# Three changes to a fused two-block kernel: one-pass gates, one-pass mean shift, and two bias rows loaded from the on-chip row

## The chip, the core and the metric

The kernel runs on one core of a Trainium2 chip. The metric is the device time of one execution in microseconds. Three executions of the kernel before took 2050.70, 2051.24 and 2051.36 us; the median is 2051.24. The profiled execution took 2050.76 us, of which the span from the first to the last instruction is 2048.9.

## What is computed

Two transformer blocks over 512 tokens of width 1024, all in float32. The parts that the change touches are these.

```python
# block 1: gated linear attention, its gates
log_a = log_sigmoid(g_low @ gla_gate_up + gla_gate_bias) / 16     # g_low: 512 x 16, gate_up: 16 x 512
# block 2, two layers: forgetting attention
log_f = log_sigmoid(f_logit + b_forget)                            # 512 x 8 heads
c = cumsum(log_f, axis=tokens)
logits = where(causal, scores + c[query] - c[key], -inf)           # per head
# block 2, after each half layer
mu = mean(x); var = mean(square(x - mu)); y = (x - mu) * rsqrt(var + eps) * g + b
```

The rest is projections, a block attention, a retention part and feed-forward products.

## The kernel before

Activations stand transposed: eight tiles of 128 channels by 512 tokens. TensorE does the large products as three one-pass products. A weight tile and an activation tile are each split into a high part, which the one-pass type float32r holds, and the low rest, and high*high + high*low + low*high is summed in PSUM (`tile`, L675 to L692, and `tile_tok`, L706 to L717). ScalarE makes the high parts of weights (L2135) and VectorE the low parts (L1273), a piece of 8 x 128 columns at a time, and `Walk` keeps pieces prepared two ahead. SyncE loads the weights into two stage buffers (L2851), each when the pieces of the buffer's old content are split.

One Python walk is run for each engine, with the same order of steps. A *tick* is one step k of a product, three matmuls. Side work (an attention, the linear attention, a norm's mean) is a generator in `w.beside`; each tick adds `w.pace` to a credit, and each whole credit runs one step of the generator. So a `yield` more is a step later on every engine. Engines work in program order, and semaphores in `on.wait_ge` hold them back.

**Gates.** After the last thin product, VectorE adds its two halves into `glow` (16 x 512), scales it (L1471), and TensorE computes the gates of one head with one float32 matmul, `gup` times `glow` (L871), four times, in steps of `gla` at pace 0.55. ScalarE and VectorE turn each into the decay factors.

**Mean shift.** The norm of block 2 keeps its sums exact by first taking off a rough mean. `norm_tile` copies tile 0 to `accq` (L1757) and adds tiles 1 to 7 (L1760) as they come. After tile 1, in the third step, `centre` multiplies the sum of two tiles by a matrix of 1/1024 in float32 (L1001), and ScalarE scales the result by 4 into `cB`, which `deviate` subtracts (L1770). There are four norms, N = 0 to 3: N = 0 and 2 behind the output product of layers 0 and 1, N = 1 and 3 behind the feed-forward product. In `last_three`, more sums and the normalisation follow.

**Bias of the forgetting attention.** VectorE makes the negative running sum of the eight heads, `lsb`, 8 partitions x 512. GpSimd writes it to `cneg` in memory (L2813), waits, and loads for each head its row, repeated over 128 partitions, into `Cb` (`load_cb`, L2803 to L2807; issue at L2806), heads 0 and 1 at once and the next ones as buffers come free. Of it and of the columns in `stat` it makes the bias of each of 32 score tiles in `bi` (L2822, L2826). VectorE adds the bias to the scores and takes the maximum (L1309), which frees the two score banks of TensorE (L774, L775); ScalarE takes the exponential (L2172), and after the normalisation and TensorE's transpose it copies the high part of the turned tile into `x_PT` (L2181). The first such additions stand on VectorE ahead of the low halves of the value tiles (L1359), and these free the banks in which the next products of TensorE begin (L686). A store of the eight tiles of H (`parked`, L2861) must be over before `Cb` is written, since they share room.

Of the kernel before, what the change touches and what calls it, by code (L numbers as in the profile page):

```python
# [7 lines left out]
F32 = mybir.dt.float32  # L8
# [487 lines left out]
def build(nc, xT, w_in, gate_up, w_bm, w_bg, w_out, w_up, w_down, w_in2, w_out2, w_ff1, w_ff2,  # L496
          consts, params, out, vrev, cneg):
    ctx = ExitStack()
    with ctx:
        base = -(-nc.sbuf_base // 64) * 64  # L500

        def at(name, off_kb, shape, dt=F32):
            return nc.alloc_sbuf_tensor_at(name, shape, dt, offset=base + int(off_kb * KB))
# [48 lines left out]
        ones = at("ones", g0 + 1, [128, 128])  # L552
        onec = at("onec", g0 + 1.5, [128, 128])
        onev = at("onev", g0 + 2, [128, 128])
# [9 lines left out]
        H = at("H", g0 + 12, [128, 8, S])  # L564
        ident, blk = cst[:, 0:128], cst[:, 128:256]
        epsc, eps5, rtok, mqs = rcol[:, 8:9], rcol[:, 9:10], rcol[:, 0:4], rcol[:, 10:11]
# [5 lines left out]
        oh = at("oh", g0 + 66, [33, 640])  # L572
        gup = at("gup", g0 + 92, [16, 512])
        sq = [at("sq0", g0 + 80, [128, S]), at("sq1", g0 + 82, [128, S])]
# [16 lines left out]
        rev = at("rev", g0 + 69, [128, 640])  # L591
        glow = at("glow", g0 + 94, [16, 512])

# [19 lines left out]
        d8 = at("d8", g0 + 36, [128, 8, S])  # L613
        acc2 = at("acc2", g0 + 70, [128, S])
        cB = at("cB", g0 + 72, [128, S])
        muB = at("muB", g0 + 74, [128, S])
# [52 lines left out]
        def tensor(e):  # L669
# [199 lines left out]
            def gates(hd):  # L869
                on.wait_ge(gup_in["in"], vec_gla["low"], *free[4])  # L870
                t = e.matmul(banks[4][:, :], gup[:, 128 * hd:128 * hd + 128], glow[:, :], start=True, stop=True)  # L871
                t.then_inc(*pe_gla.up("gate", hd))
                free[4] = [vec_gla["z", hd]]
                yield
                yield

            def gla():
                for _ in range(2):
                    yield
# [119 lines left out]
            def centre(N):  # L999
                on.wait_ge(vec_norm["acc", N, 1], *free[4])  # L1000
                t = e.matmul(banks[4][:, :], onec[:, :], accq[:, :], start=True, stop=True)  # L1001
                t.then_inc(*pe_sum.up("centre", N))
                free[4] = [act_norm["centre", N]]
# [260 lines left out]
        def vector(e):  # L1264
# [126 lines left out]
            e.tensor_copy(gmask[:, :], cm2[:, 0:128]).then_inc(*vec_x.up("gmask"))  # L1391
            e.tensor_scalar(mqs, prm[:, V_MQ:V_MQ + 1], 0.125, None, ALU.mult).then_inc(*vec_x.up("mqs"))

            moba = Heads(0)
# [66 lines left out]
            def ev_thin(dst, *events):  # L1461
# [7 lines left out]
                return evict  # L1469
            w.thin("P", nothing, ev_thin(glow[:, :]))  # L1470
            e.tensor_tensor(glow[:, :], glow[:, :], rB[0:16, :], ALU.mult).then_inc(*vec_gla.up("low"))  # L1471

# [36 lines left out]
            def gla():  # L1509
                for _ in range(2):  # L1510
                    yield
# [242 lines left out]
            def norm_tile(N, j):  # L1754
                if j == 0:
                    on.wait_ge(*h_over[0], *over("norm", N))
                    e.tensor_copy(accq[:, :], H[:, 0, :]).then_inc(*vec_norm.up("acc", N, 0))  # L1757
                else:
                    on.wait_ge(*h_over[j], vec_norm["acc", N, j - 1], *([pe_sum["centre", N]] if j > 1 else []))
                    e.tensor_tensor(accq[:, :], accq[:, :], H[:, j, :], ALU.add).then_inc(*vec_norm.up("acc", N, j))  # L1760
                if j == 1:
                    w.beside.append(spaced([nothing], 3))
                    w.pace = 1.0
                for k in DEVIATE.get(j, ()):
                    deviate(N, k, None)
# [359 lines left out]
        def scalar(e):  # L2125
# [148 lines left out]
            def ev_val(m):  # L2274
                return lambda i, c, b: w.after(2, lambda: qk_square(m))
# [7 lines left out]
            for what, j in MOBA_TILES:  # L2283
                w.gemm("P", 8, nothing, ev_val(j) if what == "val" else nothing)
            for half in range(2):
                w.tok("P", nothing, nothing)
            w.finish()
            w.thin("P", nothing, nothing)


# [18 lines left out]
            def gla():  # L2309
                for _ in range(2):  # L2310
                    yield
# [181 lines left out]
            def centre(N):  # L2493
                on.wait_ge(pe_sum["centre", N], *over("norm", N))
                t = e.activation(cB[:, :], banks[4][:, :], ACT.Copy, scale=4.0)
                t.then_inc(*act_norm.up("centre", N))
# [108 lines left out]
            for L in range(2):  # L2605
# [29 lines left out]
                def first_heads(L=L, a=a, fox=fox, ph=ph):  # L2635
                    w.beside.append(attention_order(w, fox, Attention(
                        a, fpS, fPT, [cneg_out["out", L], vec_attn["sums", L], *ph[0]], [parked["out", L]])))

# [108 lines left out]
        def gpsimd(e):  # L2747
# [52 lines left out]
            for L in range(2):  # L2800
# [10 lines left out]
                duplicate(a, 1 - L, *began)  # L2811
                on.wait_ge(vec_attn["cneg", L])
                e.dma_start(cneg[L], lsb).then_inc(*cneg_out.up("out", L, by=16))  # L2813
                load_cb(0, parked["out", L])
                load_cb(1, parked["out", L])
                for n in range(32):
# [138 lines left out]
```

## Time and profile before

| | before |
|---|---|
| median of three | 2051.24 us |
| profiled execution | 2050.76 us |
| its span | 2048.9 us |
| TensorE busy | 2024.0 us, 99% |
| VectorE, ScalarE, GpSimd busy | 64%, 50%, 18% |
| granted clock of TensorE, mean | 0.998 |
| float32 gates, L871 | 8 records for 4 matmuls |
| float32 shifts, L1001 | 8 records for 4 matmuls |

How to read it: an engine's busy time is the union of its records. TensorE's matmuls are pipelined, so a record of 0.39 us with the next one 0.23 us later is the usual picture; the cost of a matmul is read between starts. An idle time stands only where TensorE had nothing in flight.

### The profile page before, as it was taken

The page shows a single profiled execution, that of the slowest core. Times are in us where ns is not written, and L with a number is a line of the kernel's source. Part 1 is how long each engine was busy: PE and PEld are TensorE (multiplying, and loading weights), DVE is VectorE, ACT ScalarE, POOL GpSimd, SP SyncE. Part 2 cuts the span into 40 slices and gives each one's busy share as a digit, 9 for nine tenths or more (in the row PEclk, how much of TensorE's full clock was granted, in tenths as well). Part 3 has the DMA queues.
Part 4 walks back from the last instruction along what each step waited for, and adds up shares of the span by engine and source line. Part 5 has one row for each costly group of instructions (what it writes and reads, how often), then busy time and mean ns, then how long its engine had stood idle before and what let it go on. Part 6 is the DMA issues. An engine that isn't in the chain of part 4 may idle for free. (4 is left out here: it accounts for less than half of the span.)

```text
span 2048.9 us, 27766 instructions
## 1 busy us (share of the span) xinstructions
PE 2024.0 (99%) x11040; PEld 1730.9 (84%) x11040; DVE 1302.5 (64%) x2058; ACT 1020.7 (50%) x1684; POOL 371.3 (18%) x315
## 2 busy tenths in 40 slices
PE   9999999999999999999999999999999999999997
PEld 6888788888898998788788899898888788899896
DVE  6664656566774664476677575567677577566576
ACT  5664344334462543366357364464566357364363
POOL 0010000000133230254000233130354000323220
PEclk9999999999999999999999999999999999999999
DMA  7332222423232423633232242332533332242331
GB/s 245 98 108 64 83 62 83 143 95 111 90 117 73 133 66 100 181 103 103 98 104 85 81 144 62 105 122 63 166 110 90 115 93 95 65 143 62 124 104 41
DMA packets 201533, 211.58 MB, mean 103 GB/s; under 512 B 7803, under 2 KB 181115, under 8 KB 201404
## 3 DMA queue, kind: packets, MB, share of 16 engines
q1 hardware_dynamic: 194544, 194.13, 30.4%
q0 software_dynamic: 6352, 15.24, 2.8%
q8 instruction: 87, 1.43, 0.3%
q10 hardware_dynamic: 508, 0.43, 0.1%
q14 instruction: 42, 0.34, 0.1%
HBM read 194.55 MB, written 8.95 MB: 99 GB/s over the span
## 5 line engine op out<-in xcount | busy, mean ns | idle before, releaser
L686 PE MATMUL ps<-Phi,wh 128*128 128x512 f32 (+1 forms) x888 | 352.9, 397 | 3.8 <-DVE x_fvv L1359 1.3
L1273 DVE TENSOR_TENSOR wl<-stage,wh 128x1024 fp32r<-128x1024 f32 (+1 forms) x246 | 311.8, 1274 | 60.8 <-ACT wh L2135 42.1
L689 PE MATMUL ps<-Phi,wl 128*128 128x512 f32 (+1 forms) x888 | 332.1, 374 | 0.6 <-DVE wl L1273 0.6
L687 PE MATMUL ps<-Plo,wh 128*128 128x512 f32 (+1 forms) x888 | 331.4, 373 | 0.0
L2135 ACT ACTIVATE wh<-stage 128x1024 fp32r<-128x1024 f32 (+3 forms) x249 | 248.1, 1009 | 61.8 <-PE ps L689 38.9
L686 PE MATMUL ps<-Qhi,wh 128*128 128x512 f32 (+1 forms) x664 | 253.0, 381 | 0.7 <-DVE Qlo L1292 0.7
L687 PE MATMUL ps<-Qlo,wh 128*128 128x512 f32 (+1 forms) x664 | 251.6, 379 | 0.0
L689 PE MATMUL ps<-Qhi,wl 128*128 128x512 f32 (+1 forms) x664 | 251.5, 379 | 0.0
L2760 POOL TENSOR_TENSOR ws<-stage 128x1024 f32<-128x1024 f32 x20 | 54.9, 2744 | 932.2 <-PE ps L689 619.7
L686 PEld LDWEIGHTS ps<-Phi,wh 128*128 128x128 f32 x888 | 167.7, 189 | 41.0 <-issue 11.6
L689 PEld LDWEIGHTS ps<-Phi,wl 128*128 128x128 f32 x888 | 167.2, 188 | 31.8 <-DVE wl L1273 1.0
L687 PEld LDWEIGHTS ps<-Plo,wh 128*128 128x128 f32 x888 | 167.8, 189 | 27.7 <-issue 4.1
L1737 DVE TENSOR_TENSOR H<-H,ps 128x512 f32<-128x512 f32 x74 | 50.8, 687 | 175.8 <-PE ps L689 175.8
L686 PE MATMUL ps<-Qhi,wxh 128*128 128x512 f32 (+1 forms) x424 | 153.3, 362 | 0.0
L687 PE MATMUL ps<-Qlo,wxh 128*128 128x512 f32 (+1 forms) x424 | 151.4, 357 | 0.0
L689 PE MATMUL ps<-Qhi,wxl 128*128 128x512 f32 (+1 forms) x424 | 151.4, 357 | 0.0
L686 PEld LDWEIGHTS ps<-Qhi,wh 128*128 128x128 f32 x664 | 124.9, 188 | 25.3 <-DVE Qlo L1292 1.5
L687 PEld LDWEIGHTS ps<-Qlo,wh 128*128 128x128 f32 x664 | 124.9, 188 | 23.7 <-issue 0.5
L689 PEld LDWEIGHTS ps<-Qhi,wl 128*128 128x128 f32 x664 | 124.9, 188 | 23.5
L1292 DVE TENSOR_TENSOR Qlo<-f,Qhi 128x512 fp32r<-128x512 f32 x96 | 82.3, 857 | 68.6 <-ACT Qhi L2152 68.6
L1273 DVE TENSOR_TENSOR wxl<-stage,wxh 128x1024 fp32r<-128x1024 f32 (+1 forms) x90 | 116.9, 1303 | 7.3 <-ACT wxh L2135 7.2
L2135 ACT ACTIVATE wxh<-stage 128x1024 fp32r<-128x1024 f32 (+1 forms) x90 | 85.3, 964 | 36.7 <-PE ps L689 21.3
(357 smaller groups left out, 4579.2 us busy)
## 6 DMA issues: line engine op xcount, KB each, us to landing
stage<-in_w_ff SPq DMA_DIRECT2D x64, 1024.0 KB, 5.4
stage<-in_w_in SPq DMA_DIRECT2D x39, 1024.0 KB, 5.2
stage<-in_w_up SPq DMA_DIRECT2D x16, 1024.0 KB, 5.4
stage<-in_w_down SPq DMA_DIRECT2D x16, 1024.0 KB, 5.0
stage<-in_w_in SPq DMA_DIRECT2D x30, 512.0 KB, 5.2
stage<-in_w_out SPq DMA_DIRECT2D x12, 1024.0 KB, 5.0
stage<-in_w_bg SPq DMA_DIRECT2D x4, 1024.0 KB, 5.0
vrev<-H SPq DMA_DIRECT2D x2, 2048.0 KB, 14.4
```

Source lines behind the costliest of these rows:

```text
L686: e.matmul(o, hi[:, k, cs_], hi_x[:, kx, tok], start=k == 0, stop=False)
L687: e.matmul(o, hi[:, k, cs_], lo_x[:, kx, tok], start=False, stop=False)
L689: t = e.matmul(o, lo[:, k, cs_], hi_x[:, kx, tok], start=False, stop=k == nk - 1)
L1273: t = e.tensor_tensor(lo, src, hi.bitcast(F32), ALU.subtract)
L1292: t = e.tensor_tensor(lo, src, hi.bitcast(F32), ALU.subtract)
L1737: t = e.tensor_tensor(H[:, j, :], H[:, j, :], banks[b][:, :], ALU.add)
L2135: e.activation(hi, src, ACT.Copy).then_inc(*w_high.up(i))
L2760: e.tensor_tensor(ws[u][:, :, :, :], one, other, ALU.add).then_inc(*pool.up("weights", i))
```

## The change

It does three things.

1. The gates. `gup` and `glow` get copies of 80 rows in float32r, with 16 rows each at 0, 32 and 64 and zeros between: `gup3` has high, low, high, `glow3` has high, high, low. One matmul over the 80 rows sums high*high, low*high and high*low. ScalarE makes two copies of each, VectorE one subtraction and one memset of each. The low-rank row is made in `tm1` first. On all engines `gla` begins with four empty steps instead of two.
2. The mean shift. Tile 0 is copied to `first` in float32r (same place as `acc2`), and `centre` multiplies it alone, in one pass, by the matrix in float32r (1/1024); ScalarE scales by 8. The sum in `accq` begins with the addition of tiles 0 and 1.
3. The bias rows. GpSimd issues the load of head 0 straight from row 0 of `lsb`, then the write to `cneg`, then the load of head 1 from row 1 of `lsb`. Heads 2 to 7 load from `cneg` as before. ScalarE's first turned copy into `x_PT` (L2181), which writes over the place of `lsb`, now also waits for both loads.

```diff
@@ -550,7 +550,7 @@
         ones = at("ones", g0 + 1, [128, 128])
-        onec = at("onec", g0 + 1.5, [128, 128])
+        onecr = at("onec", g0 + 1.5, [128, 128], F32R)
@@ -562,7 +562,7 @@
         H = at("H", g0 + 12, [128, 8, S])
-        ident, blk = cst[:, 0:128], cst[:, 128:256]
+        ident, blk, onec = cst[:, 0:128], cst[:, 128:256], onecr[:, :].bitcast(F32)
@@ -570,7 +570,7 @@
         oh = at("oh", g0 + 66, [33, 640])
-        gup = at("gup", g0 + 92, [16, 512])
+        gup3, gup = at("gup3", g0 + 92, [80, 512], F32R), at("gup", g0 + 94, [16, 512])
@@ -589,7 +589,7 @@
         rev = at("rev", g0 + 69, [128, 640])
-        glow = at("glow", g0 + 94, [16, 512])
+        glow3 = at("glow3", g0 + 94, [80, 512], F32R)
@@ -612,6 +612,7 @@
         acc2 = at("acc2", g0 + 70, [128, S])
+        first = at("first", g0 + 70, [128, S], F32R)
@@ -867,15 +868,15 @@
             def gates(hd):
-                on.wait_ge(gup_in["in"], vec_gla["low"], *free[4])
-                t = e.matmul(banks[4][:, :], gup[:, 128 * hd:128 * hd + 128], glow[:, :], start=True, stop=True)
+                on.wait_ge(act_gla["gup"], vec_gla["gup low"], act_gla["low"], vec_gla["low low"], *free[4])
+                t = e.matmul(banks[4][:, :], gup3[:, 128 * hd:128 * hd + 128], glow3[:, :], start=True, stop=True)
...
             def gla():
-                for _ in range(2):
+                for _ in range(4):
@@ -997,8 +998,8 @@
             def centre(N):
-                on.wait_ge(vec_norm["acc", N, 1], *free[4])
-                t = e.matmul(banks[4][:, :], onec[:, :], accq[:, :], start=True, stop=True)
+                on.wait_ge(vec_norm["acc", N, 0], *free[4])
+                t = e.matmul(banks[4][:, :], onecr[:, :], first[:, :], start=True, stop=True)
@@ -1390,6 +1391,7 @@
             e.tensor_scalar(mqs, prm[:, V_MQ:V_MQ + 1], 0.125, None, ALU.mult).then_inc(*vec_x.up("mqs"))
+            e.memset(gup3[:, :].bitcast(F32), 0.0).then_inc(*vec_gla.up("gup zero"))
@@ -1467,8 +1469,17 @@
                 return evict
-            w.thin("P", nothing, ev_thin(glow[:, :]))
-            e.tensor_tensor(glow[:, :], glow[:, :], rB[0:16, :], ALU.mult).then_inc(*vec_gla.up("low"))
+            on.wait_ge(act_gla["gup"])
+            t = e.tensor_tensor(gup3[32:48, :], gup[:, :], gup3[0:16, :].bitcast(F32), ALU.subtract)
+            t.then_inc(*vec_gla.up("gup low"))
+            on.wait_ge(vec_gla["gup low"])
+            e.memset(glow3[:, :].bitcast(F32), 0.0).then_inc(*vec_gla.up("low zero"))
+            glow = tm1[0:16, :]
+            w.thin("P", nothing, ev_thin(glow, *turns_over(0)))
+            e.tensor_tensor(glow, glow, rB[0:16, :], ALU.mult).then_inc(*vec_gla.up("low"))
+            on.wait_ge(act_gla["low"])
+            t = e.tensor_tensor(glow3[64:80, :], glow, glow3[0:16, :].bitcast(F32), ALU.subtract)
+            t.then_inc(*vec_gla.up("low low"))
@@ -1507,7 +1518,7 @@
             def gla():
-                for _ in range(2):
+                for _ in range(4):
@@ -1754,10 +1765,11 @@
                     on.wait_ge(*h_over[0], *over("norm", N))
-                    e.tensor_copy(accq[:, :], H[:, 0, :]).then_inc(*vec_norm.up("acc", N, 0))
+                    e.tensor_copy(first[:, :], H[:, 0, :]).then_inc(*vec_norm.up("acc", N, 0))
                 else:
-                    on.wait_ge(*h_over[j], vec_norm["acc", N, j - 1], *([pe_sum["centre", N]] if j > 1 else []))
-                    e.tensor_tensor(accq[:, :], accq[:, :], H[:, j, :], ALU.add).then_inc(*vec_norm.up("acc", N, j))
+                    before = accq[:, :] if j > 1 else H[:, 0, :]
+                    on.wait_ge(*h_over[j], *([vec_norm["acc", N, j - 1]] if j > 1 else h_over[0]))
+                    e.tensor_tensor(accq[:, :], before, H[:, j, :], ALU.add).then_inc(*vec_norm.up("acc", N, j))
@@ -2282,10 +2294,16 @@
                 w.gemm("P", 8, nothing, ev_val(j) if what == "val" else nothing)
+            on.wait_ge(gup_in["in"], vec_gla["gup zero"])
+            e.activation(gup3[0:16, :], gup[:, :], ACT.Copy).then_inc(*act_gla.up("gup first"))
+            e.activation(gup3[64:80, :], gup[:, :], ACT.Copy).then_inc(*act_gla.up("gup"))
...
             w.thin("P", nothing, nothing)
+            on.wait_ge(vec_gla["low"])
+            e.activation(glow3[0:16, :], tm1[0:16, :], ACT.Copy).then_inc(*act_gla.up("low first"))
+            e.activation(glow3[32:48, :], tm1[0:16, :], ACT.Copy).then_inc(*act_gla.up("low"))
@@ -2307,7 +2325,7 @@
             def gla():
-                for _ in range(2):
+                for _ in range(4):
@@ -2492,7 +2510,7 @@
                 on.wait_ge(pe_sum["centre", N], *over("norm", N))
-                t = e.activation(cB[:, :], banks[4][:, :], ACT.Copy, scale=4.0)
+                t = e.activation(cB[:, :], banks[4][:, :], ACT.Copy, scale=8.0)
@@ -2634,7 +2652,7 @@
                     w.beside.append(attention_order(w, fox, Attention(
-                        a, fpS, fPT, [cneg_out["out", L], vec_attn["sums", L], *ph[0]], [parked["out", L]])))
+                        a, fpS, fPT, [cneg_out["out", L], Cb_in[0][L, 0], Cb_in[1][L, 1], vec_attn["sums", L], *ph[0]], [parked["out", L]])))
@@ -2809,10 +2827,12 @@
                 duplicate(a, 1 - L, *began)
-                on.wait_ge(vec_attn["cneg", L])
-                e.dma_start(cneg[L], lsb).then_inc(*cneg_out.up("out", L, by=16))
-                load_cb(0, parked["out", L])
-                load_cb(1, parked["out", L])
+                on.wait_ge(vec_attn["cneg", L], parked["out", L])
+                for h in range(2):
+                    src = bass.AP(tensor=lsb.tensor, offset=S * h, ap=[[S, 1], [0, 128], [1, S]])
+                    e.dma_start(Cb[h][:, :], src).then_inc(*Cb_in[h].up(L, h, by=16))
+                    if h == 0:
+                        e.dma_start(cneg[L], lsb).then_inc(*cneg_out.up("out", L, by=16))
```

## Rows read from the trace of the kernel before

**Rows 1.** The page, section 1: busy us (share of span) xinstructions, by engine.
```profile
PE 2024.0 (99%) x11040; PEld 1730.9 (84%) x11040; DVE 1302.5 (64%) x2058; ACT 1020.7 (50%) x1684; POOL 371.3 (18%) x315
```

**Rows 2.** TensorE timeline, 211:214, around the gate: start, us, engine, line, op, shapes, count.
```profile
211.24 0.39 PE L689 MATMUL ps<-Phi,wl 128*128 128x512 f32 x1
...
211.69 0.39 PE L687 MATMUL ps<-Plo,wh 128*128 128x512 f32 x1
211.92 0.39 PE L689 MATMUL ps<-Phi,wl 128*128 128x512 f32 x1
...
213.62 0.40 PE L687 MATMUL ps<-Plo,wh 128*128 128x512 f32 x1
```

**Rows 3.** Timeline of TensorE, 2002 to 2005, around the fourth shift (L1001, not shown).
```profile
2002.39 0.39 PE L689 MATMUL ps<-Qhi,wxl 128*128 128x512 f32 x1
...
2003.71 0.40 PE L687 MATMUL ps<-Qlo,wxh 128*128 128x512 f32 x1
```

**Rows 4.** Timeline, 1654.5 to 1658: VectorE's copy, TensorE's third shift, in brackets idle and releaser.
```profile
1654.64 0.43 DVE L1757 COPY accq<-H 128x512 f32<-128x512 f32 x1
...
1655.06 0.39 PE L689 MATMUL ps<-Qhi,wl 128*128 128x512 f32 x1
...
1655.85 1.12 PE L1001 MATMUL ps<-accq,onec 128*128 128x512 f32 x2 [0.40 <-DVE accq L1760]
...
1657.04 0.40 PE L687 MATMUL ps<-Qlo,wh 128*128 128x512 f32 x1
```

**Rows 5.** Timeline of VectorE, 1040 to 1110, after the first shift.
```profile
1054.90 0.69 DVE L1734 SCALAR_TENSOR_TENSOR H<-H,ps 128x512 f32<-128x512 f32 x1 [0.55 <-PE ps L689]
```

**Rows 6.** Timeline of GpSimd, 850 to 872 and 1455 to 1482.
```profile
852.77 0.54 POOL L2813 DMA_DIRECT2D cneg<-x_z  x1 [7.88 <-DVE x_z L1968]
854.85 1.14 POOL L2806 DMA_DIRECT2D x_Cb<-cneg  x2 [1.54 <-DMA cneg<-x_z]
860.05 0.60 POOL L2822 TENSOR_SCALAR x_bi<-x_Cb,stat 128x128 f32<-128x128 f32 x1 [4.06 <-DMA x_Cb<-cneg]
...
1462.38 0.54 POOL L2813 DMA_DIRECT2D cneg<-x_z  x1 [8.94 <-DVE x_z L1968]
1466.09 1.14 POOL L2806 DMA_DIRECT2D x_Cb<-cneg  x2 [3.17 <-DMA cneg<-x_z]
1471.04 0.60 POOL L2822 TENSOR_SCALAR x_bi<-x_Cb,stat 128x128 f32<-128x128 f32 x1 [3.82 <-DMA x_Cb<-cneg]
```

**Rows 7.** Timelines of VectorE and TensorE, 868 to 869 and 1472 to 1480.
```profile
868.05 0.69 DVE L1359 SCALAR_TENSOR_TENSOR x_fvv<-ps,x_fvv 128x512 fp32r<-128x512 f32 x1
...
868.90 0.46 PE L686 MATMUL ps<-Phi,wh 128*128 128x512 f32 x1
...
1472.66 0.44 PE L774 MATMUL ps<-f0kh,f0qs 128*128 128x384 f32 x1 [0.59 <-DVE stat L1309]
...
1479.88 0.47 PE L686 MATMUL ps<-Phi,wh 128*128 128x512 f32 x1 [1.34 <-DVE x_fvv L1359]
```

**Rows 8.** DMA digits and GB/s in 40 slices: 1445:1465; 102.2:107; 853:854.7.
```profile
DMA  0004589998999999999999999899999999999841
GB/s 0 0 4 41 94 287 311 385 295 193 295 402 393 422 410 414 377 377 377 393 381 373 393 361 307 176 225 234 324 389 348 328 273 270 286 259 270 235 125 45
...
DMA  0000000000798993059997789998999963000000
GB/s 0 0 0 0 0 0 0 0 0 0 171 290 171 188 205 69 0 119 205 256 239 137 154 171 239 239 205 188 222 239 256 188 137 69 17 0 0 0 0 0
...
GB/s 24 12 24 12 0 0 0 0 0 0 0 0 0 0 0 0 0 0 0 0 145 48 49 49 48 0 48 0 0 0 0 0 0 0 0 0 0 0 0 0
```

**Rows 9.** Timelines of SyncE and ScalarE, 854 to 866.
```profile
854.83 1.00 SPq L2851 DMA_DIRECT2D stage<-in_w_in  x2
...
865.30 1.04 ACT L2135 ACTIVATE wh<-stage 128x1024 fp32r<-128x1024 f32 x1
```

**Rows 10.** Timeline of ScalarE, 1480 to 1490.
```profile
1482.28 0.26 ACT L2181 ACTIVATE x_PT<-ps 128x128 fp32r<-128x128 f32 x1
```

## The prediction

> **What bounds the kernel now.** I read the page's busy shares first: TensorE is busy in 99% of the span [rows 1], so a change counts by what it takes off TensorE's own stream, or by what it does to the few gaps in it. Next I read TensorE's timeline at the lines that the change touches, measuring from start to start, because the matmuls' ends are modelled and overlap. Then I read the few rows of TensorE that carry an idle time, and for those the engine that released them: VectorE at two of the four mean shifts [rows 4], and VectorE twice at the start of the second layer's attention [rows 7]. The last view is of the DMA engines, since the change has them read the bias row from another place.
>
> **The gates (four matmuls, L871).** In the plain stream two matmuls take 211.69 - 211.24 = 0.45 us. From the matmul before a gate to the second after it (211.92 to 213.62) is 1.70 us [rows 2]. So an fp32 gate costs 1.70 - 0.45 = 1.25 us. The new gate is one fp32r matmul of the same 512 columns over 80 rows, 0.23 us at the pitch of its neighbours. Saved: 1.02 us each, 4.1 us in all.
> No row shows an fp32r matmul over 80 rows. The fp32 shift over 128 rows costs 2003.71 - 2002.39 - 0.45 = 0.87 us [rows 3], 0.38 less than the gate over 16 rows with the same columns; if that 0.38 is the price of few rows and 80 still count as few, the saving is 1.02 - 0.38 = 0.64 each, 2.6 in all. An end below that has no ground: one pass replaces a product that takes several. I take 4.1, as 80 rows are nearer to 128 than to 16.
> The Trainium skill's page "TensorEngine Tiling (Array Packing)", section "Key Properties", says that changing the tiling mode drains TensorE, and its list of modes has 32, 64 and 128 rows. By that 16 rows fall in another mode than the 128-row stream and 80 don't, and the sum stays as it is; the 0.38 us agrees with a drain, though the row doesn't show its cause.
> What the gates add: on VectorE two memsets, two subtractions of at most 16x512; on ScalarE four copies of 16x512. On either engine that is 0.5 to 0.7 us apiece by their 512-column neighbours. The weights' row splits are done before the attention's tail, and the low-rank row's splits stand between its product and the first gate. For these the first gate now comes two steps later: at 0.55 steps a tick and 0.68 us a tick (three matmuls at 0.23) that is 2.5 us, against two copies and one subtraction, some 2.0 us. I cost them at nothing on TensorE; without that cover it would be a wait of at most 2.0 us once. Behind ScalarE's new wait for the low-rank row stands its next weight piece, behind VectorE's wait for the copies three memsets and the low half of one; TensorE holds two pieces prepared ahead, 5.5 us each.
>
> **The shift (four matmuls, L1001).** An fp32 shift costs 0.87 us in the stream [rows 3], a one-pass one 0.23: 0.64 each, 2.5 us in all. Two of the four also wait: 1655.06 to 1657.04 is 1.98 us where the free one takes 1.32 [rows 4], so 0.66 is a wait for the sum of two tiles; the other (layer 0) is the same to 0.01. Now it waits for the copy alone, which ends at 1655.07 [rows 4], ahead of the 1655.29 at which TensorE is there. If the copy to the one-pass type takes as long as an addition (0.69 instead of 0.43) it is 0.1 us late. Both waits are worth 1.3 us. In layer 0 part of it has no use: VectorE, which everything in the norm goes through next, has only 0.55 us idle before its next tile [rows 5], of 0.64 + 0.66 = 1.3 that TensorE would bring; 0.7 comes back as a wait later. Shift together: 2.5 + 1.3 - 0.7 = 3.1 us. Taking one tile's sum and 8 instead of two and 4 adds no instruction.
> So the two TensorE edits are worth 4.1 + 3.1 = **7.2 us**, between 5 and 8.
>
> **The bias rows (two layers).** GpSimd writes the row to memory at 852.77, issues the two loads when it has landed (854.85) and starts the first bias at 860.05; in layer 1 at 1462.38, 1466.09 and 1471.04 [rows 6]. The change drops the hop: load 0 goes out at 852.77 and 1462.38, then the write to memory, then load 1. Without anything else the first bias comes 2.1 and 3.7 us earlier. What is late next, if so, is nothing: in layer 1 TensorE's idle 0.59 and 1.34 us go [rows 7], in layer 0 there was none.
> But the load now has 128 readers of one partition. Three rows bound what that costs. With all partitions taking part and the engines full (digit 9) they move up to 422 GB/s, some 25 per engine. The copies from 64 partitions to 64 move 188 to 290 at digit 9, mostly near 230, a little over half. The write from 8 partitions runs at 49 GB/s [rows 8]. So the pace falls with the partitions touched. 256 KB (262144 bytes) would take 5.3 us at 49 GB/s, and 43 us if one of the eight partitions gives an eighth of it. Between these ends I take one engine's pace, 25 GB/s, which is 10.4 us: it is also half of what the eight partitions give, and the row nearest to the case is theirs. With 1.8 us for the way (2.1 from issue to use for the write, less 0.3 for its bytes) load 0 is in 12.2 us after its issue: at 865.0 and 1474.6, so 4.9 and 3.5 us **later** than before.
> The Trainium skill's page "SBUF — State Buffer", section "Door 1: The DMA port swizzle", speaks against this edit: eight partitions share one port, and a transfer over partitions 0 to 3 was measured at 27.6 GB/s. That gives an estimate of 9.5 us instead of 10.4 for the row, and a sum 1.8 us lower than mine (0.9 in each layer). The rows on 8 and on 64 partitions agree with it; none here has a single one.
> TensorE feels it through VectorE, which works in order: its bias additions stand ahead of the value tiles that free TensorE's banks. In layer 0 that value tile is done at 868.74 and TensorE needs it at 868.90 [rows 7], 0.1 to 0.2 of cover; in layer 1 it is already late. The price is 4.8 + 3.5 = **8.3 us**. Load 1 lands 10.4 later than load 0. The fifth bias wants it, behind four of GpSimd's, and now ScalarE too, before its first turned copy: in layer 1 at 1482.28 [rows 10] + 3.5 = 1485.8, against 1462.38 + 1.8 + 20.8 = 1485.0. I count it as covered, by 0.8 us; at a slower pace this wait, with the exponentials and value tiles queued behind it, becomes the longer one, and each us on a row costs two. The loads for the heads from 2 on find the row in memory as before. GpSimd's joint wait for the parked tiles isn't new (the load waited for them).
>
> **Sum.** The profiled execution took 2050.76 us (span 2048.9), 0.5 below the median of 2051.24. 2050.8 - 7.2 + 8.3 = 2051.9 on that one, 2052.3 against the median.
>
> **Rivals.**
> A, the row is read as fast as memory (5.2 us from issue to use, as now) or at 49 GB/s (5.3 + 1.8 = 7.1). For it: the engines read repeated rows of memory without trouble. Against it: the half-height copies. Then layer 0 pays nothing and layer 1 gets back its 1.9 us (1.6 at 49 GB/s): 2051.2 - 7.2 - 1.9 = 2042.1.
> B, slower: the readers hold the DMA engines, and the weights wait behind them. Place: weights issued at 854.83 are turned by ScalarE at 865.30 [rows 9], ahead of the value tiles on its queue. The two row loads hold the engines to 852.77 + 1.8 + 2 x 10.4 = 875.4; ScalarE would want the weights at 865.30 + 4.9 = 870.2, so it stands 5.2 us, and in layer 1 about as long. It decides from a landing some 15 us after that issue, instead of before 865. Price 10.4: 2052.3 + 10.4 = 2062.7.
> C, one pass saves less than counted (the first gate waits 2.0 us, or 80 rows still pay): 2054 to 2056, with the row as forecast.
>
> **Chances.** Forecast 0.50, its own range 2048 to 2057; A 0.27; B 0.16; C 0.07. A measurement of this kernel can tell about 0.2%, 4.1 us: faster is below 2047.1, slower above 2055.3. Faster: A's 0.27 and 0.03 of the forecast's low end = 0.30. Slower: B's 0.16, 0.04 of C, 0.13 of the forecast's high end (the row at under 21 GB/s, or half of B) = 0.33. The rest, 0.37, is within 0.2%. The range for 8 in 10 is 2041 to 2062: it takes in A, and B up to its full price. It leaves out a row at an eighth of 49 GB/s.
>
> **What would show it.** Right: gates and shifts with one record of about 0.4 us and 0.45 us to the second matmul after plus 0.23; no idle before a shift in either layer; load 0 of each layer with a landing near 12 us, TensorE idle at the third score product and at the first matmul after the value tiles, 4.8 us in layer 0. Wrong: a landing of 3 to 7 us (A), ScalarE idle on a stage of weights near 870 and 1480 (B), unhidden weight loads around the gates or TensorE idle at the first gate (C). The biggest error to expect is in the 10.4 us: 1 us more in each layer is 2 us of the whole.

## The result, and the profile after

The changed kernel takes 2075.41 us (median of 4, 2074.93 to 2076.61) against 2051.22 us (2050.70 to 2051.36): 24.2 us **slower**, ratio 1.012 (95% interval 1.0108 to 1.0131). The forecast was 2052.3, and the range 2041 to 2062 doesn't hold the time. The profiled execution took 2075.08 us (span 2073.3, mean granted clock 0.993).

The two TensorE edits did on TensorE what they should. First the page's busy times, then TensorE's timeline around the first gate (L872) and the fourth shift (L1002); columns are start, us, engine, line, operation, shapes, count.

```profile
PE 2022.1 (98%) x11032; PEld 1733.5 (84%) x11032; DVE 1305.7 (63%) x2062; ACT 1023.7 (49%) x1688; POOL 369.0 (18%) x315
```

```profile
215.19 0.39 PE L690 MATMUL ps<-Phi,wl 128*128 128x512 f32 x1
215.42 0.40 PE L872 MATMUL ps<-glow,gup 80*128 80x512 f32 x1
215.65 0.40 PE L687 MATMUL ps<-Phi,wh 128*128 128x512 f32 x1
...
2027.17 0.39 PE L690 MATMUL ps<-Qhi,wxl 128*128 128x512 f32 x1
2027.40 0.39 PE L1002 MATMUL ps<-first,onec 128*128 128x512 f32 x1
2027.62 0.39 PE L687 MATMUL ps<-Qhi,wxh 128*128 128x512 f32 x1
2027.85 0.39 PE L688 MATMUL ps<-Qlo,wxh 128*128 128x512 f32 x1
```

The gate over 80 rows takes 0.23 us of the stream, as any matmul of 512 columns (before 1.25 [rows 2]); the shift too (2027.85 - 2027.17 = 0.68, before 1.32 [rows 3]). TensorE is busy for 1.9 us less and yet ends 24.4 later, so it is idle for 26.3 us more. Most of that, 22.6 us, is in four rows, two in each attention, where the kernel before has 0, 0, 0.59 and 1.34 us [rows 7]:

```profile
864.42 0.44 PE L775 MATMUL ps<-f0kh,f0qs 128*128 128x384 f32 x1 [2.78 <-DVE stat L1310]
...
880.17 0.76 PE L687 MATMUL ps<-Phi,wh 128*128 128x512 f32 x1 [9.88 <-DVE x_fvv L1360]
...
1487.67 0.69 PE L775 MATMUL ps<-f0kh,f0qs 128*128 128x384 f32 x1 [3.90 <-DVE stat L1310]
...
1502.88 0.76 PE L687 MATMUL ps<-Phi,wh 128*128 128x512 f32 x1 [7.93 <-DVE x_fvv L1360]
```

The two waits of a pair have different causes. The **first wait** is that of a late bias. GpSimd's timeline in both layers answers to [rows 6]:

```profile
850.92 0.57 POOL L2833 DMA_DIRECT2D x_Cb<-x_z  x1 [7.88 <-DVE x_z L1980]
851.48 0.56 POOL L2835 DMA_DIRECT2D cneg<-x_z  x1
852.01 0.59 POOL L2833 DMA_DIRECT2D x_Cb<-x_z  x1
862.80 0.60 POOL L2842 TENSOR_SCALAR x_bi<-x_Cb,stat 128x128 f32<-128x128 f32 x1 [10.20 <-DMA x_Cb<-x_z]
...
1474.07 0.57 POOL L2833 DMA_DIRECT2D x_Cb<-x_z  x1 [8.93 <-DVE x_z L1980]
...
1486.05 0.60 POOL L2842 TENSOR_SCALAR x_bi<-x_Cb,stat 128x128 f32<-128x128 f32 x1 [10.31 <-DMA x_Cb<-x_z]
```

From GpSimd's first issue to its first bias it is 11.9 and 12.0 us, against 7.3 and 8.7 before: 4.6 and 3.3 us late. The **second wait** is behind ScalarE, which stands on a stage of weights with the value tiles queued behind it:

```profile
876.58 1.06 ACT L2147 ACTIVATE wh<-stage 128x1024 fp32r<-128x1024 f32 x1 [8.43 <-DMA stage<-in_w_in]
...
1499.28 1.06 ACT L2147 ACTIVATE wh<-stage 128x1024 fp32r<-128x1024 f32 x1 [7.90 <-DMA stage<-in_w_in]
```

Before, ScalarE had that stage at 865.30 without a wait [rows 9]. What happened to it is in the DMA view of two stretches of layer 0, 852.9 to 862.4 and 872 to 877 (mean busy share of the 16 engines in tenths, 40 slices, then what they moved; q0 is GpSimd's queue, q1 the one with the weights). It is also in the landing times, that is the time from a load's issue until all of it has arrived, of the row loads (L2833) and of the three weight loads issued from 853 on (L2871):

```profile
DMA  6009699909600596990990056999099000699908
GB/s 17 0 0 34 17 34 69 52 0 52 17 0 0 17 34 17 86 52 0 34 34 0 0 17 17 34 52 86 0 34 34 0 0 9 26 43 52 78 0 26
DMA packets 102, 0.26 MB, mean 27 GB/s; under 512 B 36, under 2 KB 36, under 8 KB 102
q0 software_dynamic: 102, 0.26, 90.5%
...
DMA packets 2346, 1.63 MB, mean 326 GB/s; under 512 B 35, under 2 KB 2345, under 8 KB 2345
```

```profile
DMA to landing us min/median/max: 11.8/15.9/20.1
...
DMA to landing us min/median/max: 12.1/20.9/23.2
```

For 9.5 us all 102 packets are GpSimd's. They take up 90.5% of the time of 16 engines and move 27 GB/s. (The digits have gaps, since a packet of 4 KB is longer than a slice; q0's share is the number to read.) Not one packet of weights moves in that stretch, though two loads of them were issued at its start. Load 0 lands 11.8 us after its issue, load 1 after 20.1, so at 862.7 and 872.1: 9.4 us apart for 256 KB, 28 GB/s. From 862.4 to 870.3 it is much the same: q0 takes 90.8%, and 0.02 MB of weights move. Only as load 1 runs out do the weights come in, 0.3 MB before 872 and 1.63 MB in the 5 us shown, and ScalarE goes on at 876.58.

After the long waits TensorE also runs at its lower clock for a while. The stretches 866 to 870, 870 to 880, 880 to 883 and 883 to 890 (busy time and count by engine, then the granted clock, the DMA share, GB/s):

```profile
866.00:870.00 4.00, 4.00 (x19) 3.19 (x17) 1.58 (x4) 0.60 (x2) 3.42 (x4) 1.00 0.97 32
870.00:880.00 10.00, 0.29 (x2) 0.00 (x0) 2.28 (x5) 2.49 (x5) 0.41 (x1) 0.65 0.73 210
880.00:883.00 3.00, 2.83 (x8) 2.17 (x8) 2.41 (x7) 2.96 (x7) 1.53 (x4) 0.50 0.20 60
883.00:890.00 7.00, 7.00 (x37) 5.85 (x36) 3.57 (x11) 4.18 (x10) 4.58 (x5) 0.99 0.59 162
```

0.50 is the 1.2 GHz level. Matmuls start every 0.43 us there instead of 0.23, seven of them: 1.4 us. In layer 1 it is more, since both waits are followed by such a stretch, again at a granted 0.50: seven matmuls after the 3.90 us and eleven after the 7.93 us. In all TensorE is busy for 5.8 us longer than in e3 below, which has the same one-pass products and the rows through memory (2022.1 against 2016.3).

### The profile page after: what moved, and what is told of

The parts are those of the page before. It is cut to its first block and busy times, and to the rows that moved or that the text cites. A ratio compares the mean times of both kernels' runs of the same rounds, so it can differ in the third digit from the quotient of the medians.

```text
span 2073.3 us, 27759 instructions
## 1 busy us (share of the span) xinstructions
PE 2022.1 (98%) x11032; PEld 1733.5 (84%) x11032; DVE 1305.7 (63%) x2062; ACT 1023.7 (49%) x1688; POOL 369.0 (18%) x315
```

## The experiments

The theory after the result: the loss is the bias rows' alone, with two prices, the late first bias and the DMA engines held by a read of one partition. The rivals: only the lateness, or a disturbance from the one-pass edits. Times are medians in us. What a run from e5 on costs is counted from e3 (2046.82), also where its code differs from the changed kernel's. In e6, e7, e13, e14 and e17 the bias of one or both of the heads 0 and 1 is left out, so they show only time.

| run | what | us | ratio to before (95%) |
|---|---|---|---|
| e1 | gates alone | 2048.51 | 0.9988 (0.9979 to 0.9997) |
| e2 | shift alone | 2049.93 | 0.9992 (0.9983 to 1.0001) |
| e3, e15 | gates and shift | 2046.82, 2046.62 | 0.998 (0.9971 to 0.9988), 0.998 (0.9972 to 0.9989) |
| e4 | bias rows alone | 2079.53 | 1.0138 (1.0124 to 1.0152) |
| e5 | head 0's row alone from the chip | 2056.67 | 1.0029 (1.0018 to 1.004) |
| e6, e14 | both loads from 8 neighbours | 2053.78, 2055.0 (one run) | 1.0014 (1.0005 to 1.0024) |
| e17 | one load from 8 neighbours | 2048.01 (one run) | |
| e13 | both from 8 partitions, 16 apart | 2047.50 | 0.9981 (0.9972 to 0.999) |
| e7 | both from 128 partitions | 2044.69 | 0.9972 (0.9961 to 0.9984) |
| e8 | e3 and two reads nobody waits for | 2069.33 | 1.009 (1.0075 to 1.0105) |
| e9 | e3 and a late first bias | 2055.90 | 1.0026 (1.0017 to 1.0035) |
| e10, e16 | e3, 128 columns from the chip | 2045.92, 2045.45 | 0.9976 (0.9967 to 0.9985), 0.9972 (0.9961 to 0.9983) |
| e11 | e3, 128 columns first, from memory | 2047.41 | 0.9984 (0.9975 to 0.9992) |
| e12 | e3, gates two steps earlier | 2047.99 | 0.9989 (0.998 to 0.9998) |

### Which edit carries the loss (e1 to e4)

e1 takes the parts of the diff that touch `gup`, `glow` and the empty steps of `gla`, e2 those on `first`, `onec` and the scale, e3 both. e4 takes the rest, against the kernel before:

```diff
-                e.dma_start(cneg[L], lsb).then_inc(*cneg_out.up("out", L, by=16))
-                load_cb(0, parked["out", L])
-                load_cb(1, parked["out", L])
+                for h in range(2):
...
+                    e.dma_start(Cb[h][:, :], src).then_inc(*Cb_in[h].up(L, h, by=16))
+                    if h == 0:
+                        e.dma_start(cneg[L], lsb).then_inc(*cneg_out.up("out", L, by=16))
```

> The kernel before with the one-pass gates alone. Theory (from the trace after): a gate costs 0.23 us instead of 1.25, 4.1 us in all, but about 1.3 to 1.6 us comes back as waits for VectorE at the norm products of the last heads (1.08 and 0.26 us idle seen in the trace after): 2051.2 - 2.6 = 2048.6. Rival (my forecast): nothing comes back, 2047.1. Rival 2: the gates bring nothing here, because what follows was bound by VectorE: 2050.5 to 2051.2.

> The kernel before with the one-pass shift alone. Theory: 0.64 us each in four places and two waits of 0.66 us gone, 1.0 back in layer 0 as a wait of the next product of the same norm (L1013): 2051.2 - 2.9 = 2048.3. My forecast was 3.1: 2048.1. Rival: the norms are bound by VectorE in both layers, so it saves under 1 us: over 2050.2.

> Gates and shift in one pass, the bias rows through memory as before. If the whole loss is the rows' (theory): 2051.2 - 5.5 = 2045.7, between 2044.5 and 2047. Rival, the one-pass edits carry a part of the 24 us: above 2051. My forecast for this part was 7.2 us: 2044.0.

> The bias rows of heads 0 and 1 from the chip alone, gates and shift as before. Theory: all of the loss and the part that the other two edits gave back: 2075.4 + 5.5 = 2081, layer 0 and layer 1 each losing 12 to 15 us on TensorE. Rival, my forecast: 8.3 us, 2059.5. Rival 2, TensorE's earlier arrival through the faster gates and shift is what made the waits long, so that part of the loss is missing here: 2070 to 2078.

Measured: -2.4, -1.0, -4.1 and +28.6 us against the kernel before (2050.95 in these runs). The changed kernel stands 28.6 above e3 too. So the rows carry the whole loss, whatever TensorE does elsewhere, and the one-pass edits are a gain of 4.1. In e4 TensorE's four waits are 2.81, 8.23, 3.87 and 7.55 us, as in the changed kernel. e2 was a miss, 1.0 for 2.9. Its trace shows why: TensorE at the next product of the same norm, and ScalarE 10 us ahead of it:

```profile
1071.84 0.80 PE L1014 MATMUL ps<-accq,onec 128*128 128x256 f32 x1 [2.36 <-DVE accq L1794]
...
1061.32 1.06 ACT L2137 ACTIVATE wh<-stage 128x1024 fp32r<-128x1024 f32 x1 [1.85 <-DMA stage<-in_w_ff]
```

That TensorE is ahead doesn't make the weights land sooner. The piece they hold up stands ahead of the residual tiles on VectorE's queue, and the wait comes back at the product. It was 0.62 us in e3, 0.82 in e15, 1.11 in the changed kernel, 2.45 in e16 and none before, where ScalarE waited 0.51, 0.41, 0.75, 1.92 and 0 for that weight load. So it goes with the landing of those weights, and layer 0's part of the shift's gain comes and goes with it.

### Late bias or held engines (e5, e8, e9)

e5, against the changed kernel, head 1 through memory:

```diff
-                for h in range(2):
...
+                e.dma_start(Cb[0][:, :], src).then_inc(*Cb_in[0].up(L, 0, by=16))
+                e.dma_start(cneg[L], lsb).then_inc(*cneg_out.up("out", L, by=16))
+                load_cb(1)
```

e8, against e3, two idle reads of partition 0 of a table, written to unused memory. GpSimd waits for them ahead of its twelfth bias, which in layer 0 comes at 902.85, 28 us after they have landed, so this wait costs nothing:

```diff
+                for k in range(2):
+                    t = e.dma_start(unused[k], bass.AP(tensor=src.tensor, offset=src.offset, ap=[[2 * S, 1], [0, 128], [1, S]]))
...
+                    if n == 11:
+                        on.wait_ge(idle_in[L, 1])
```

e9, against e3, GpSimd busy ahead of its first bias:

```diff
+                for k in range(5):
+                    e.tensor_scalar(bi[1][:, :], tab[:, 0, :], 0.0, None, ALU.add).then_inc(*pool.up("busy", L, k))
+                    on.wait_ge(pool["busy", L, k])
```

> The changed kernel, but only head 0's row comes from the chip; head 1's load goes through memory, once the row's copy has landed there. Theory (two prices: the row is late by 4.6 and 4.2 us, and each load from one partition holds all 16 DMA engines for some 10 us, so that two of them make the weights late): the engines are free by 862.5, the weights issued at 853 land by some 869, so the long waits of 9.9 and 7.9 us go and the lateness stays, with 1.4 us more for each layer as the first bias stands behind the copy's landing: 2046.8 + 8.8 + 2.8 = 2058, between 2054 and 2062. Rival (the holding of the engines isn't the cause; the late first bias makes all of it): 2074 to 2079.

> Gates and shift in one pass and the rows through memory (2046.8), and behind the two loads of each layer two more, which nobody waits for: 128 readers of one partition of a table, 256 KB each, written to unused memory. The first bias isn't late here; only the engines are held, from 856 to about 877. Theory: the weights issued at 862.5 and later land near 878 instead of 868, ScalarE stands on them some 8 us in each layer: 2046.8 + 16 = 2063, between 2056 and 2069. Rival (the weights' queue gets its turns between the slow packets, and the loss in the changed kernel is the row's lateness): 2046.8 to 2049.

> Gates and shift in one pass, rows through memory (2046.8), and behind the two loads of each layer GpSimd copies a 128x512 table five times into a tile it overwrites later, 1.6 us each, before its first bias. No slow read is anywhere; only the first bias comes late, by 3.9 us in layer 0 and about 5 in layer 1, close to what the row load makes it (4.6 and 4.2). Theory: TensorE pays the lateness one for one, less 0.2 of cover in layer 0: 2046.8 + 8.7 = 2055.5, close to the 2056.7 of the run with one row load, and no wait above 5 us at the value tiles. Rival (a late first bias disturbs the order of the queues and so makes the 8 to 10 us waits by itself): above 2065.

e9 (late, nothing held) costs 9.1 us: in layer 0 GpSimd's first bias is at 861.58 instead of 857.71 and TensorE's first matmul after the value tiles at 870.42 instead of 866.56, **3.9 for 3.9**. The other 5.2 are layer 1's, for a bias 4.1 us late; there the matmuls after the wait of 5.31 us run at the lower clock, and TensorE is busy for 2.8 us more than in e3 (2019.1 against 2016.3). The 8 to 10 us waits aren't there; 5.31 is the largest. e5 (late, and one load held) costs 9.9, about the same, and has no wait at the value tiles: with the engines free after one load the weights come in time. e8 (held, not late) costs 22.5. The first bias is at 857.75, on time, and yet ScalarE and TensorE stand. Here are ScalarE in both layers, TensorE in layer 0, and the landing of the idle reads (layer 0, L2837):

```profile
875.95 1.06 ACT L2147 ACTIVATE wh<-stage 128x1024 fp32r<-128x1024 f32 x1 [12.85 <-DMA stage<-in_w_in]
...
1505.32 1.06 ACT L2147 ACTIVATE wh<-stage 128x1024 fp32r<-128x1024 f32 x1 [7.16 <-DMA stage<-in_w_in]
...
879.54 0.77 PE L687 MATMUL ps<-Phi,wh 128*128 128x512 f32 x1 [12.72 <-DVE x_fvv L1360]
...
DMA to landing us min/median/max: 12.8/16.8/20.7
```

That settles it: two reads that no bias depends on cost 22.5 us. The two prices overlap (9.1 + 22.5 = 31.6, both together 28.6), since a late first bias also moves the moment at which ScalarE asks for the weights, from 863.1 in e8 to 868.1 in the changed kernel. In layer 0 the overlap is whole: TensorE's waits are 12.72 us in e8 and 2.78 + 9.88 = 12.66 in the changed kernel. e8 came out 6 us above what I expected. The weights landed at 875.9, not later than the 878 I had, but they were those issued at 853 and not those of 862.5, and ScalarE asked for them at 863.1. So it stood 12.85 and 7.16 us instead of 8 in each layer. The lower clock comes on top: TensorE is busy for 4.9 us more than in e3.

### What makes the read slow (e6, e7, e13, e14, e17)

e6 and e14; e17 the same in e5's form:

```diff
+                    src = bass.AP(tensor=lsb.tensor, offset=0, ap=[[S, 8], [0, 16], [1, S]])
```

e7:

```diff
+                    src = tab[:, 0, :]
```

e13:

```diff
+                    src = bass.AP(tensor=t0.tensor, offset=t0.offset, ap=[[16 * 2 * S, 8], [0, 16], [1, S]])
```

> The changed kernel, but both loads read eight partitions (0 to 7), 16 readers each, instead of one partition with 128; same bytes, same destinations. Left out: the bias of heads 0 and 1 is wrong by it, their attention isn't the reference's. Theory A, each partition has its own pace (27 GB/s for one, about 49 or more for eight, as the row's copy to memory ran): landing 7 us or less after the issue, engines free by 862: 2045 to 2050. Theory B, the eight neighbours share one way out, so eight are no faster than one: landing 12 and 20 us, 2075 as the changed kernel. Rival C, the copy from chip to chip by this queue is slow whatever it reads: 2075 too, and then the next run is slow as well.

> The changed kernel, but both loads read 128 partitions (a table of 128x512), one reader each; same bytes, same packets, same destinations. Left out: the bias of heads 0 and 1 is that table. Theory (the single partition is slow): landing within 2 to 5 us, the first bias before 857, no loss, and layer 1's waits of 0.59 and 1.34 us gone: 2043.5 to 2046.8. Rival C (chip to chip is slow on this queue whatever is read): landings of 12 and 20 us and 2075.

> The changed kernel with both loads reading eight partitions 16 apart (0, 16, ... 112 of a table), 16 readers each; same bytes and packets. Left out: the bias of heads 0 and 1 is that table. Theory (neighbouring partitions share one way out, so eight apart have eight of it): both land within 3 to 5 us and the time is that of the run with 128 partitions, 2044 to 2047. Rival (only the number of partitions counts): like eight neighbours, landings of 11 us and 2053.8.

> A second look at both loads from eight neighbouring partitions (0 to 7), as the run of that name; the bias of heads 0 and 1 is wrong by it. If the pace is a property of the source and not of that chip, the landings are 11.4 and 11.8 us again and the time 2053 to 2055; if not, anything between 2046 and 2075.

> The changed kernel with head 0's load from eight neighbouring partitions (0 to 7, 16 readers each) and head 1's load through memory behind the row's copy: one slow load instead of two. Left out: head 0's bias is wrong by it. Theory (the two loads shared the pace of about 48 GB/s of the neighbourhood): the one load lands 1.7 + 5.4 = 7.1 us after its issue, and the time is near 2050. Rival (a load from there has 27 GB/s of its own, whatever else runs): 11.4 us again, and near 2056 as with the one row.

Landings in layer 0 (from the issue), of e6, e17, e13 and e7 in this order; e17 has one such load, the others two:

```profile
DMA to landing us min/median/max: 11.4/11.4/11.5
...
DMA to landing us min/median/max: 7.1/7.1/7.1
...
DMA to landing us min/median/max: 5.6/6.0/6.5
...
DMA to landing us min/median/max: 2.3/2.4/2.5
```

Same bytes, same queue, same destination. From one partition the two loads are in 21.2 us after the first issue, from eight neighbours 12.6, from eight far apart 7.6, from 128 partitions 3.6. So it isn't a copy within the chip that is slow, and it isn't only the number of partitions: eight apart are about twice as fast as eight neighbours, which are about twice as fast as one. Both of my theories for e6 fell (neither as slow as one nor eight times as fast), and in e13 the loads came in at about twice the neighbours' pace, not eight times one partition's. e17 shows why e6's first load was no sooner than from one partition: the two loads shared the pace, and one alone lands after 7.1 us, as its theory had it (its time, a single run, is 2 us under the 2050 expected). e14 repeats e6's source and its landings (11.5 and 11.6 in layer 0).

The Trainium skill gives a reason that fits, on the page "SBUF — State Buffer", section "Door 1: The DMA port swizzle". A port serves four partitions and the four that lie 32 further on. So one partition is on one port, 0 to 7 are on two, and 0, 16, ... 112 are on four, at about 27 GB/s each. The pace measured here agrees: 28 GB/s from one partition (256 KB in the 9.4 us between the landings), 48 from eight neighbours (both loads, 512 KB in the 12.6 us less 1.8 of way), and a mean of 108 in e13's stretch 851.5 to 854.5. That it is the ports and not something else about neighbours isn't shown: no run read eight partitions of one port (0 to 3 and 32 to 35), or changed the port with nothing else.

### What could still be had (e10, e11, e12, e15, e16)

e10 and e16, against e3: after the row's copy to memory is issued:

```diff
+                head = bass.AP(tensor=lsb.tensor, offset=0, ap=[[S, 1], [0, 128], [1, 128]])
+                e.dma_start(Cb[0][:, 0:128], head).then_inc(*idle_in.up("head", L, by=16))
...
+                t = e.dma_start(Cb[0][:, 128:], bass.AP(tensor=src.tensor, offset=src.offset + 128, ap=[[0, 128], [1, S - 128]]))
```

e11, the same, but the head comes from `cneg[L]`, behind the wait for `cneg_out`:

```diff
+                head = bass.AP(tensor=cneg[L][0:1, :].tensor, offset=cneg[L][0:1, :].offset, ap=[[0, 128], [1, 128]])
+                on.wait_ge(parked["out", L], cneg_out["out", L])
```

e12, against e3, in `gla` on all three engines:

```diff
-                for _ in range(4):
+                for _ in range(2):
```

> Gates and shift in one pass; of head 0's row only the first 128 columns (all that the first bias needs) come from the one partition, 64 KB instead of 256, behind the row's copy to memory; the rest and head 1's row through memory. Theory (time goes by the bytes read from the partition): this piece moves in a quarter of 10.1 us and lands 1.7 + 2.5 = 4.2 us after its issue, the first bias comes 2 to 3 us earlier, the second not later than 1 us: 2045.5 to 2048. Rival (a fixed price of some 10 us for any read of one partition by 128): landing near 12, as late as the whole row, 2056 or more.

> As the run before, but the first 128 columns also come through memory, as a load of their own ahead of the rest: nothing reads one partition. Theory (in layer 1 the start of the attention waits for the first biases, 1.38 and 1.34 us idle on TensorE): the small load lands about 1 us sooner, part of that idle goes: 2045 to 2047. Rival (the time of a load is its way and not its bytes, or the third bias is the one that counts): 2046.8, no change, or up to 1 us more for the extra issue on GpSimd.

> Gates and shift in one pass, but the gated heads start after two empty steps, as in the kernel before, instead of four. The low-rank row's second split ends at 213.6 in the changed kernel, the gate would come at about 212.9. Theory (the four steps cover the splits, and the 1.35 us at the last heads' norm products come from VectorE's queue there): TensorE waits about 1 us at the first gate, 2047 to 2048. Rival (the two steps more are what pushed the last heads' norm products into VectorE's way): the 1.35 us go and little comes for it, 2045.5 to 2046.

> Gates and shift in one pass, rows through memory, again, on the same chip as the next run: 2046.8, 4 us under the kernel before.

> The same with the first 128 columns of head 0's row from the one partition. If the earlier gap is real it is 0.5 to 1.5 us faster than the run before, with the idle of 1.38 us at layer 1's third score product gone and 1.34 us at the value tiles down to 0.4. If it was the chip, within 0.4 us of it.

The 64 KB piece from the one partition lands after 4.1 to 4.5 us, the 256 KB row after 11.8: the price goes by the bytes. GpSimd's first bias in layer 0 of e10 is at

```profile
855.29 0.60 POOL L2846 TENSOR_SCALAR x_bi<-x_Cb,stat 128x128 f32<-128x128 f32 x1 [1.57 <-DMA x_Cb<-x_z]
```

where e3 has it at 857.71, and layer 1's waits are 0.43 instead of 1.38 + 1.34 (in e16 none). The time is 0.9 and, on one chip, 1.2 us under e3's and e15's, in the same direction both times, but the intervals overlap. With nothing of the computation left out it is the fastest kernel here, 5.5 us under the kernel before in e16. The same piece through memory (e11) brings nothing that can be told: it goes out only after the hop, and the one more issue pushes the second bias to 860.22 (e3: 858.84).

In e12 the gate comes too early for its operand:

```profile
213.34 0.47 PE L872 MATMUL ps<-glow,gup 80*128 80x512 f32 x1 [0.92 <-DVE glow L1481]
```

TensorE waits 0.92 us for the low-rank row's second split, and two smaller waits follow in the next heads, where e3 has 1.07 and 0.27 us at the last heads' norm products. The median is 1.2 us above e3's. The intervals of the two overlap and they ran on different chips, so the time alone shows no gain of the four empty steps; the trace shows that they cover the splits. e11's 0.6 us above e3 is no difference either.

## Why the prediction was wrong

Point by point, in the order of the forecast.

- **Gates: right in price, not in worth.** 1.02 us each, 4.1 in all, is what TensorE's stream gives (0.23 after 1.25), and 80 rows pay nothing extra. But e1 gained 2.4. The step that failed is that I cost the gates' additions to the other engines at nothing on TensorE and looked only at the first gate. TensorE now stands at two norm products of the last heads, 1.3 us in all, where it stood at none:

```profile
272.10 1.12 PE L932 MATMUL ps<-sq,onev 128*128 128x512 f32 x2 [1.08 <-DVE sq L1555]
...
296.57 1.12 PE L932 MATMUL ps<-sq,onev 128*128 128x512 f32 x2 [0.26 <-DVE sq L1555]
```

- **Shift: right in price, its cover mis-sized.** 0.64 us each and 1.3 for the two that also waited (1680.29 to 1680.98, 0.69, before 1.98 [rows 4]) stand. Of layer 0 I let 0.7 us come back, from VectorE's free 0.55 [rows 5]. Measured were 0.6 to 2.4, and the wait goes with a weight load's landing and not with VectorE's free time. Together the one-pass edits are worth 4.1 us (e3) and 4.3 (e15), where I had 7.2 and at the least 5: 3.1 us of the sum's error.
- **Load 0: right in time, by luck in its ground.** My 12.2 us from issue to use, 10.4 of them at 25 GB/s, were 11.9 and 12.0, and the bias is 4.6 and 3.3 us late instead of 4.9 and 3.5. But I took 25 GB/s as the pace of one engine. The trace shows the reads taking 90.5% of the time of all 16, so another limit happened to give the same number, and what it did to the engines I had wrong. TensorE pays lateness one for one in layer 0 (e9), as the 0.1 to 0.2 us of cover said. In layer 1 e9's 4.1 us of lateness cost 5.2, a part of it at the lower clock. The term I had at 8.3 is about 9. Load 1 was covered, as counted: ScalarE's first turned copy waits 0.36 and 0.66 us in the two layers, both times for TensorE and not for a load.
- **Held engines: the step that failed.** Forecast and sum rest on the sentence that load 1 costs nothing because its reader comes late enough. That asks only who waits for the load, not who shares the engines with it. Rival B said it, with its place right (ScalarE on the weights issued after the row loads, value tiles behind it), but I gave it 0.16. The rows would have told: the half-height copies run at digit 9 with 188 to 290 GB/s [rows 8]. I read them as a pace. Digit 9 at half the throughput says more: a slow transfer fills the engines' time as a fast one does. Two loads that fill 16 engines for 20 us leave no room for the 1 MB of weights issued at their start. ScalarE wanted the second half of it at 868.1 and had it at 876.6.
- **B's own price was too low**, 10.4 us for both layers and 2062.7, where the whole loss is 28.6 less the 9 of lateness. Its end of the holding was about right (22.6 us after the first issue; load 1 landed 1.1 + 20.1 = 21.2 us after it, at 872.1), and so was the moment at which ScalarE wants the weights. Left out was that the weights still have to come in after load 1, 1.63 MB in 5 us: ScalarE stood 8.43 and 7.90 us instead of 5.2 in each layer, 5.9 more. Left out was also the lower clock after the long waits, which makes TensorE busy for 5.8 us more than in e3. With both, and its one-pass term 3.1 us too good, B comes to 2062.7 + 5.9 + 5.8 + 3.1 = 2077.5, against 2075.41 measured. So about 2 us are too much in the rest; I can't say where, as the prices of lateness, holding and clock overlap.
- **Rival A** (as fast as memory) is out, and e7 says what it would have been worth. With both loads from 128 partitions the first bias is at 853.20, and the kernel is at 2044.7, 2.1 under e3, close to the 1.9 us I had for layer 1 (the intervals of e7 and e3 overlap). **Rival C** is half right, in size but not in mechanism: the first gate doesn't wait and 80 rows don't pay.

The Trainium skill's page "DMA: Bandwidth & Descriptors", section "Queues, rings and completion order", says that each DMA engine takes turns between its queues, a packet at a time. By that rule the weights would have had their turn between the row's slow packets. The trace shows no such turns: of the 102 packets between 852.9 and 862.4 none was theirs, though their loads were issued at 853. A packet in that section is typically 9 to 17 descriptors and may be more than one of the trace's. But after load 0 too, from 862.4 to 870.3, only 0.02 MB of weights moved. Where they were held up stays open. SyncE's second issue at 853.4 itself took 6.42 us, where the two issues in the kernel before took 1.00 together [rows 9]. That can't be all of it: in e8 the two issues also took 1.00 us and came before the slow reads, and yet the second load landed 22.9 us after its issue.

## What to carry to other kernels

Before a transfer is moved off memory, ask from how many partitions it reads and how far apart they lie; the row that 128 readers want was better fetched from memory, all 256 KB of it, than from the one partition that has it. Look in the trace whether a slow transfer keeps all DMA engines busy, as here. If it does, cost it as their time, and add what has queued up behind it, even where its own reader comes late. If the row must come from the chip, take only the columns that the first reader needs: here the time went by the bytes. And an idle time of TensorE can cost more than itself, by the lower clock behind it.

## What the hardware showed that I had not expected

- Reads of one partition by 128 readers ran at 28 GB/s, of eight neighbours at 48, of eight partitions 16 apart at a mean of 108, while the DMA engines counted as busy.
- Two reads of one partition that no bias waits for cost 22.5 us (e8), more than twice as much as a bias 4 us late in each layer (9.1, e9).
- After the wait of 9.88 us TensorE was granted 0.50 of its clock for about 3 us.
- With the shift in one pass TensorE waits 0.6 to 2.4 us at a later product of layer 0 that stood behind no wait before (the most in e2 and e16), more than the 0.7 counted in most of them.
